# Opening block of a hybrid decoder layer: x loaded ahead of the weights, high halves ahead of squares, diagonal from PSUM, gating products first

## What is computed

```
h = concatenate([meta, x], axis=1)               # 1040 tokens x 1024
u = rmsnorm(h, norm_w)                           # x * rsqrt(mean(x*x) + EPS) * w
proj = einsum('btd,dc->btc', u, w_in)            # 1024 -> 4104 columns
... = split(proj)    # hg_q hg_f hg_i hg_z | gd_qkv | gd_z | gd_a gd_b
g    = -exp(A_log) * softplus(gd_a + dt_bias)    # per head and token
beta = sigmoid(gd_b)
gam  = cumsum(g)                                 # over the chunk
```

## Time and profile before

| what | value |
|---|---|
| median of three runs | 800.14 us (799.35 to 805.16) |
| the profiled execution | 804.47 us |
| its span | 802.8 us |
| PE busy | 730.1 us (91%) |
| DVE, ACT, POOL busy | 458.0, 305.6, 339.3 us |
| opening block | PE's last matmul of it starts at 89.53 us |

### The profile page before, as it was taken

The page is one execution under the profiler, slowest core; times in us unless marked ns, Lnnn a source line. Parts: engine busy times, 40 slices in busy tenths (PEclk is TensorE's granted clock), DMA queues, the critical chain, the costliest instruction groups (busy, mean ns, idle before and its releaser), DMA issues. The chain is left out here.

```text
span 802.8 us, 13601 instructions
## 1 busy us (share of the span) xinstructions
PE 730.1 (91%) x4851; PEld 692.0 (86%) x4851; DVE 458.0 (57%) x1011; ACT 305.6 (38%) x782; POOL 339.3 (42%) x449
## 2 busy tenths in 40 slices
PE   6799898999998989999989899999898949999975
PEld 6789898989998989899989898999898937888764
DVE  4928344378881444788814437888144266865146
ACT  4635523534544226245442253454422232232133
POOL 3671332166552321665533216655333055754124
PEclk9899999999999999999999999999999977999998
DMA  8525224230222256714354423022243042211005
GB/s 215 81 32 79 27 31 75 28 51 3 40 51 43 31 68 33 41 14 33 50 34 48 75 27 52 2 41 45 48 111 71 13 151 99 92 47 47 1 27 210
DMA packets 77031, 45.54 MB, mean 57 GB/s; under 512 B 30894, under 2 KB 72212, under 8 KB 76964
## 3 DMA queue, kind: packets, MB, share of 16 engines
q1 hardware_dynamic: 76964, 44.66, 32.9%
HBM read 36.41 MB, written 8.24 MB: 56 GB/s over the span
## 5 line engine op out<-in xcount | busy, mean ns | idle before, releaser
L221 PE MATMUL proj<-uTh,w_high 128*128 128x352 f32 (+1 forms) x768 | 263.5, 343 | 11.6 <-POOL w_low L239 5.4
L221 PE MATMUL proj<-uTh,w_low 128*128 128x352 f32 (+1 forms) x768 | 246.8, 321 | 0.0
L221 PE MATMUL proj<-uTl,w_high 128*128 128x352 f32 (+1 forms) x768 | 246.6, 321 | 0.0
L221 PEld LDWEIGHTS proj<-uTh,w_high 128*128 128x128 f32 x768 | 145.6, 190 | 13.8 <-issue 7.2
L221 PEld LDWEIGHTS proj<-uTl,w_high 128*128 128x128 f32 x768 | 145.6, 190 | 0.0
L221 PEld LDWEIGHTS proj<-uTh,w_low 128*128 128x128 f32 x768 | 144.8, 189 | 0.0
L239 POOL TENSOR_TENSOR w_low<-w_raw,w_high 128x256 fp32r<-128x256 f32 (+1 forms) x54 | 70.5, 1306 | 29.3 <-ACT w_high L231 29.3
L1505 PE MATMUL mix<-level_x 128*128 128x128 f32 x448 | 67.1, 284 | 9.7 <-issue 4.3
L1505 PEld LDWEIGHTS mix<-level_x 128*128 128x128 f32 x448 | 62.3, 197 | 14.6 <-issue 13.1
L1147 POOL TENSOR_TENSOR f_suffix<-f_suffix,f_prefix 128x192 f32<-128x192 f32 x84 | 56.2, 669 | 22.1 <-DVE f_prefix L1334 14.2
L1344 DVE COPY_PREDICATED hg_scores<-mask_st,mix 128x384 f32<-128x384 uint8 (+1 forms) x96 | 52.0, 542 | 18.8 <-PE mix L1505 18.3
(11 more groups left out here) (307 smaller groups left out, 1409.3 us busy)
## 6 DMA issues: line engine op xcount, KB each, us to landing
w_raw<-in_w_in SPq DMA_DIRECT2D x32, 512.0 KB, 8.3
x_tile<-in_x SPq DMA_DIRECT2D x8, 512.0 KB, 7.2
w_raw<-y_scratch SPq DMA_DIRECT2D x8, 384.0 KB, 4.3
decay<-gamma_scratch SPq DMA_DIRECT2D x4, 576.0 KB, 4.0
landing<-in_w_out SPq DMA_DIRECT2D x4, 512.0 KB, 7.6
landing<-in_x SPq DMA_DIRECT2D x3, 512.0 KB, 3.5
y_scratch<-gd_y SPq DMA_DIRECT2D x6, 192.0 KB, 1.8
decay<-in_w_out SPq DMA_DIRECT2D x2, 512.0 KB, 3.7
```

The costliest lines, as they stand in the source:

```text
L221: last = pe.matmul(acc[:, 0:tw], w[j % 2][:, k, :], u[:, k, t0:t0 + tw], start=(k == 0 and i == 0), stop=(k == KT - 1 and i == 2))
```

## The change

Line numbers with L are of the kernel before; in the rows of order for the kernel after, the numbers are its own (L398, L490, L498, L594, L605, L652, L739 and L755 are there what L400, L493, L501, L597, L608, L655, L756 and L744 are before).

- SP: all x tiles and `gate_raw` are issued ahead of the first weight tile and the two small broadcasts `A_log`, `dt_bias`.
- ACT: in round i the two high halves come before the square of tile i+3. `gate_h` is made in round 5 instead of 6. The first weight tile's high part comes behind all of u instead of in round 4.
- POOL: `ones` and `pmask` are made before the loop; the first `early_low` is behind the loop instead of in round 4.
- PE: one more transpose at the start puts the identity in PSUM (`ident_ps`, in the last bank of the ring); the diagonals are made from it. `gate_piece(0)` is put behind x tile 6, ahead of tiles 7 and 8; pieces 1 and 2 follow tile 8; every projection follows them.
- DVE: `gate_l` is made after half 13 instead of 14; `decay_diff` is ahead of `conv_taps(1)`.

```
-    BESIDE = {6: range(0, 3), 7: range(3, 6), 8: range(6, 2 * PARTS)}
+    ident_ps = bank[5][:, 384:384 + P]
...
-            for i in range(2, 5):
-                load_x(i)
-            load_tile(0, tile_cols("gd", GD_KINDS[0], 0))
-            sp.dma_start(pr[:, 0, :], A_log[0:1, :].broadcast_to([P, HEADS])).then_inc(prm_in, 16)
-            sp.dma_start(pr[:, 1, :], dt_bias[0:1, :].broadcast_to([P, HEADS])).then_inc(prm_in, 16)
-            for i in range(5, XS):
+            for i in range(2, XS):
                 load_x(i)
             sp.dma_start(gate_raw[:, :, :], w_in_v[:, :, AB_COLS:AB_COLS + 2 * HEADS]).then_inc(gate_in, 16)
             for i in range(XS, NC):
                 full(sp, front, ("x", i - XS, 1))
                 load_x(i)
+            load_tile(0, tile_cols("gd", GD_KINDS[0], 0))
+            sp.dma_start(pr[:, 0, :], A_log[0:1, :].broadcast_to([P, HEADS])).then_inc(prm_in, 16)
+            sp.dma_start(pr[:, 1, :], dt_bias[0:1, :].broadcast_to([P, HEADS])).then_inc(prm_in, 16)
...
                 low_part(pool, 2 * i + 1)
-                if i == 4:
-                    early_low(0)
...
+            early_low(0)
...
             for i in range(NC):
-                if i + AHEAD < NC:
-                    square_tile(i + AHEAD)
                 if i == 0:
...
                 for half in range(2):
                     high_part(2 * i + half)
-                if i == 4:
-                    early_high(0)
-                if i == 6:
+                if i + AHEAD < NC:
+                    square_tile(i + AHEAD)
+                if i == 5:
                     act.wait_ge(gate_in, 16)
                     act.copy(gate_h, gate_raw[:, :, :]).then_inc(gate_high, 1)
...
+            early_high(0)
+            take_gate(0)
...
-                dve.tensor_scalar(diag[i % DIAGS][0:w, 0:w], ident[0:w, 0:w], rstd[0:w, i:i + 1], None,
+                dve.tensor_scalar(diag[i % DIAGS][0:w, 0:w], ident_ps[0:w, 0:w], rstd[0:w, i:i + 1], None,
...
-                if n == 14:
+                if n == 13:
                     dve.wait_ge(gate_high, 1)
...
+            def gate_piece(g):
+                t0, tw = PIECES[g]
+                for low in u_low:
+                    pe.wait_ge(low, 1 + -(-(t0 + tw - META) // P))
+                pe.wait_ge(gate_low, 1)
...
+            pe.transpose(ident_ps, ident[:, :], ident[:, :]).then_inc(ident_there, 1)
...
-                project(BESIDE.get(i, ()))
...
+                if i == 6:
+                    gate_piece(0)
+            gate_piece(1)
+            gate_piece(2)
+            project(range(0, PARTS))
...
-            project(range(3 * PARTS, 5 * PARTS))
+            project(range(PARTS, 3 * PARTS))
```

More of the change, by code:

```diff
@@ L340, in hybrid_layer @@
         sq_done, rstd_done, scaled = sem("sq_done"), sem("rstd_done"), sem("scaled")
-        cleared, u_high = sem("cleared"), sem("u_high")
+        cleared, u_high, ident_there = sem("cleared"), sem("u_high"), sem("ident_there")
         u_low = [sem("u_low_dve"), sem("u_low_pool")]
@@ L417, in _ @@
             pool.tensor_copy(mask_st[:, 0, :], ident[:, :]).then_inc(consts, 1)
+            pool.memset(ones[:, :], 1.0).then_inc(ones_set, 1)
+            pool.memset(pmask[:, :], 1.0).then_inc(pm0, 1)
+            pool.wait_ge(pm0, 1)
+            pool.affine_select(out=pmask[:, :], in_=pmask[:, :], compare_op=ALU.is_ge, fill=0.0,
+                               base=-PAD, pattern=[[1, 1]], channel_multiplier=1).then_inc(pm0, 1)
             def early_low(n):
@@ L538, in _ @@
                     high_part(2 * i + half)
-                if i == 4:
-                    early_high(0)
-                if i == 6:
+                if i + AHEAD < NC:
+                    square_tile(i + AHEAD)
+                if i == 5:
                     act.wait_ge(gate_in, 16)
                     act.copy(gate_h, gate_raw[:, :, :]).then_inc(gate_high, 1)
-                    act.wait_ge(prm_in, 32)
-                    act.activation(ea[:, :], pr[:, 0, :], ACT.Exp).then_inc(gate_exp, 1)
-            take_gd_front(act, 0, split=False)
[L547 to L553, removed]
+            early_high(0)
+            take_gate(0)
+            act.wait_ge(prm_in, 32)
+            act.activation(ea[:, :], pr[:, 0, :], ACT.Exp).then_inc(gate_exp, 1)
+            take_gate(1)
+            take_gate(2)
+            early_high(1)
+            take_gd_front(act, 0, split=False)
             act.wait_ge(gate_step, 3)
@@ L557, in _ @@
             act.activation(gw[:, 5, :, :], gw[:, 3, :, :], ACT.Ln, bias=1.0).then_inc(gate_exp, 1)
+            take_gd_front(act, 1, split=False)
+            take_gd_front(act, 2, split=False)
+            early_high(2)
+            first_tap(0)
             take_gd_front(act, 3, split=False)
-            take_gd_front(act, 4, split=False)
             act.wait_ge(gate_step, 12)
@@ L563, in _ @@
             act.activation(cols[:, :, 4, :], gw[:, 2, :, :], ACT.Exp).then_inc(gate_exp, 1)
+            take_gd_front(act, 4, split=False)
             take_gd_front(act, 5, split=False)
@@ L636, in _ @@
             last.then_inc(mask_set, 1)
-            dve.wait_ge(const0, 4)
+            dve.wait_ge(ident_there, 1)
             for i in range(AHEAD - 1):
@@ L710, in _ @@
             dve.tensor_scalar(cols[:, :, 5, :], cols[:, :, 0, :], -1.0, None, ALU.mult)
-            conv_taps(1)
             for g in range(NG):
                 decay_diff(dve, 0, g, dec_in, dec_sub)
+            conv_taps(1)
             dve.wait_ge(mask_step, 2 * LEVELS)
@@ L731, in project @@
                     project_part(pe, n, 1)
+            def gate_piece(g):
[3 more added lines that the diff above has]
+                pe.wait_ge(gate_low, 1)
+                if g >= 2:
+                    pe.wait_ge(gate_out, g - 1)
+                for k in range(KT):
+                    for n, u in enumerate((uh, ul)):
+                        last = pe.matmul(gbank[g % 2][0:4 * HEADS, 0:tw], gate_w[:, k, :], u[:, k, t0:t0 + tw],
+                                         start=(k == 0 and n == 0), stop=(k == KT - 1 and n == 1))
+                last.then_inc(gate_done, 1)
+            pe.wait_ge(const0, 4)
+            pe.transpose(ident_ps, ident[:, :], ident[:, :]).then_inc(ident_there, 1)
             pe.wait_ge(rows_in, 80)
-            pe.wait_ge(const0, 4)
             ap, done = take(pe, front, "rows")
@@ L775, in _ @@
             pe.matmul(ap[:, 0:HEADS * NC], ones[:, :], g_all, start=True, stop=True).then_inc(done, 1)
-            project(range(5 * PARTS, 5 * PARTS + 3))
+            project(range(3 * PARTS, 3 * PARTS + 3))
             pe.wait_ge(gate_step, 10)
@@ L779, in _ @@
             pe.transpose(ap[0:HEADS * NC, 0:P], gam[:, :, :].rearrange("p h c -> p (h c)"), ident[:, :]).then_inc(done, 1)
-            project(range(5 * PARTS + 3, 4 * len(PIECES) * PARTS))
+            project(range(3 * PARTS + 3, 4 * len(PIECES) * PARTS))
     end_block()
```

## The result

The changed kernel takes 811.99 us (median of 4 runs, 810.58 to 812.91), the kernel before 801.91 us in the same comparison: ratio 1.0115, 95% interval 1.0089 to 1.014. It is about 1% slower; 809.4 us was forecast. The profiled execution took 812.34 us with a span of 810.5 us.

The account below looks back on a forecast made before the run. PE was taken to bound the opening block, from the date it never waits again. G at 49.4 less break-even 40.1 gave +9.3 us on the 800.14 median: 809.4 us, with 801.5 to 815.5 for 8 in 10 runs.

Parts of the forecast that it names:

- Break-even at 40.1 us: Opening block: it stays as long as before if the last half of u has its low part at 40.1 us.
- G: Date when the last half of u has its low part, before which nothing is projected; forecast 49.4 us.
- G + 10.1: PE after G: gating piece 2 (2.42 us) and two projection pieces (7.7 us), reaching where it was at 50.26.
- The ring: Loop over ACT, POOL and DVE: square behind high halves closes a one-round chain, 4.18 us a round; before 3.29.
- The wait of `gate_l` for POOL: DVE after norm(12): `gate_l` ends with POOL's low(13), putting gate_low 3.4 us after norm(12), at 37.4 us.
- The low clock: PE idle over 7 us: gating matmuls at 0.32 us, high clock back 6.1 us after work resumes, at 43.5.
- my low end: Low end of the sum, +5.1 us: `gate_l` in front (-1.2) and the high clock all through (-3.0).
- Sum: Opening block: 49.4 - 40.1 = +9.3 us, giving 809.4 us against the median, 1.2% slower.
- An open ring with the gating piece in place: Rival: ring doesn't close or has slack, clock stays high; rounds 2.3 us, G = 36.6, 796.6 us; chance 0.15.
- A diagonal from PSUM that waits for POOL: Rival on DVE: +5.5 us more, or low clock past tile 8, +5; 815 us; chance 0.1 for either.
- `gate_l` in front: DVE: `gate_l` issues ahead of POOL's low(13), gate_low at 36.3 instead of 37.4; -1.2 in the low end.
- That x arrives earlier bought nothing: Loads: the ring doesn't ask for tile 5 before 19.1 us, and it arrives at 18.80 already; no gain.

Follow-up runs that it names:

- squares first: Changed kernel with ACT's old order back: the square of tile i+3 ahead of the high halves of tile i; 800.73 us, ratio 0.9973.
- squares alone further ahead: Changed kernel with squares and rstd one tile further ahead (AHEAD 4), diagonals left at tile i+2; 803.05 us, ratio 0.9988.
- closed in the kernel before: Kernel before with only the new ACT order: high halves of tile i ahead of the square of tile i+3; 807.65 us, ratio 1.007.
- `AHEAD` alone: Changed kernel with AHEAD 4 instead of 3, moving squares and diagonals together; 810.38 us, ratio 1.0081.
- The fastest kernel with its identity in SBUF: Changed kernel with old ACT order and first gating piece behind x tile 8, diagonals made from SBUF as before; 797.67 us, ratio 0.9924.
- the run with 70 transposes: Changed kernel with 70 unused identity transposes on PE between x tile 6 and the first gating piece; 810.27 us, ratio 1.0086.
- the fastest kernel: Changed kernel with ACT's old order back and the first gating piece behind x tile 8; 795.02 us, ratio 0.9905.
- gating behind x: Changed kernel with its first gating piece behind x tile 8 on PE instead of ahead of tiles 7 and 8; 805.43 us, ratio 1.0024.
- with 34: Changed kernel with 34 unused identity transposes on PE between x tile 6 and the first gating piece; 812.87 us, ratio 1.0124.
- the identity in PSUM alone: Kernel before with one more PE transpose putting the identity in PSUM and the diagonals made from it; 802.61 us, ratio 0.999.

## Why the prediction was right

**Break-even at 40.1 us: right.** G came out at 48.32 us (the start of the last gating piece), 48.3 - 40.1 = +8.2, and the block is 8.29 us longer. Nothing behind the gating was late: PE goes from the last gating matmul (50.59) straight to the first projection (50.74). The third piece starts at 59.39, 1.0 us behind G + 10.1, because the transposes of the gating now precede it (0.7 us) instead of following.

**The ring: right, a little too short.** 4.32 us instead of 4.18. Two links were longer: square to diagonal 2.20 us (19.10 to 21.30) for 2.15, and diagonal to norm 0.27 (21.30 to 21.57) for 0.20, the second being the PSUM source, 0.35 us against 0.29. Four rounds of that make norm(12) 34.52 us instead of 34.0, from the same start: norm(4) is at 17.26, as forecast (17.29), although norm(3) did not wait for PE until 13.70 in this run. The ring is shown by the runs: opened in two ways (squares first, squares alone further ahead) the round is 2.2 to 3.2 us from tile 5 on, closed in the kernel before it is 5.17, and `AHEAD` alone leaves it at 4.32.

**The wait of `gate_l` for POOL: wrong.** I took gate_low at 37.4 by the row at 24.29 us; it was 36.49 + 0.22 = 36.71. By the rule of the Trainium skill ("SBUF — State Buffer", "Who interferes with whom") DVE, 0.04 us ahead of POOL, goes first, and so it was:

```profile
36.49 0.22 DVE L652 TENSOR_TENSOR gate_split<-gate_raw,gate_split 128x64 fp32r<-128x64 f32 x1
```

```profile
36.53 1.31 POOL L398 TENSOR_TENSOR uTl<-u_part,uTh 128x512 fp32r<-128x512 f32 x1 [1.15 <-ACT uTh L490]
```

The fastest kernel with its identity in SBUF has both outcomes at a lead of 0.03 us, so neither the row nor the rule decides so close a case by the recorded starts. From norm(12) to gate_low I had put 3.4 us; it took 34.52 to 36.71, 2.19 us. The term was 1.2 us too large, and as the ring made norm(12) 0.5 us later than forecast, the date was off by 0.7 only.

**The low clock: right in kind, its end mis-sized.** It came back at about 41.95 us, 5.1 us after PE began again, not 6.1, and a gating matmul took 0.29 us, not 0.32. So the gating piece took 4.65 us for 5.1, and tiles 7 and 8 3.7 us for 3.9. Against everything at the high clock it cost 2.0 to 2.3 us (the run with 70 transposes); my low end had 3.0 for it.

**Sum.** +9.3 us forecast, +8.3 by the traces' dates, +10.1 by the medians of the first comparison. Later comparisons put the kernel before at 804.0 to 804.4 us, 2.1 to 2.5 us above its first median, which would account for the difference: 811.99 - 804.2 = 7.8 (the changed kernel was timed in the first comparison alone). The 1.1 us by which G was forecast too late is a sum of misses that partly cancel: +0.5 for the ring, -1.2 for gate_low, -0.7 for the clock, and +0.3 in small ones.

**The rivals.** An open ring with the gating piece in place would have given 796.6 us, 3.5 us faster than before. Opened by the squares first, with the gating piece in place, it made the block 1.2 us shorter (800.73 us): norm(12) was at 24.57 and gate_low at 26.76, about as this rival had them (24.3 and 27.7), but its other condition, the high clock, did not hold. With the gating piece out of the way as well it gave 795.02. A diagonal from PSUM that waits for POOL did not come: 0.35 us in every round. (Its price was also read a little high: of the five diagonals of rounds 2 to 6 before, four take 1.22 to 1.40 us and the one at 14.90 us takes 0.28. The sum did not use it. And `gate_l` in front is worth 37.4 - 36.3 = 1.1 us, not the 1.2 in the low end.) That x arrives earlier bought nothing in the changed kernel, as forecast; in the fastest kernel tile 5 is squared at 13.92 us, which the old loads (18.80) would not have allowed; what the loads are worth there was not tried by itself.

## What to carry to other kernels

When an instruction is moved in an in-order queue, count the rounds in the chain that leads from it back to itself, over all engines: a chain that closes within one round sets the round to its sum, however idle each engine is, and shows as equal waits in a ring (here 2.0, 2.0 and 2.2 us). Deepening a look-ahead helps only if it adds a round between the two ends of that chain; here moving both ends together did nothing. And an instruction that waits for a slow engine should not stand ahead of work that is ready: it cost 4.1 us with the ring closed and 6.6 us with it open (90.15 - 83.53), of which the low clock that followed PE's idle time took a part.

## What was not expected of the hardware

The granted clock also fell while PE was at work: with gating behind x, PE had 2.02 us of x products and 2.29 us of idle time per round, and the clock went to half at about 36.2 us, 0.6 us into tile 8, and before that at about 19.1 us, in tile 4, which took 3.00 us; tile 5 took 3.61. In the kernel after, with the same rhythm, it stayed at 1.00 until PE had been idle from 28.7 to about 31.7 us. The two runs with transposes, the same program up to 28.7 us, differ as well: with 34 the clock fell at 22.2 us, with 70 it did not fall in the block. So a fall of this kind is not set by the program alone, and with one trace per kernel, part of what a single date shows (the 4.10 us of the gating piece behind x above all) may be its doing. The gain of an edit of 1 us can be lost to a fall of the clock, as perhaps with the identity in PSUM alone. A transpose of 128x128 took 0.114 us at the high clock, about as long as one of the two records of an x product.
